# Prompt attention: bias addition and maximum in one VectorE operation (an addition with a running minimum, on negated queries and tables)

## The chip, the cores and the metric

The kernel runs on one core of one Trainium2 chip. The metric is the device time of one execution in microseconds (us), the median of several runs. The profile that is quoted below is of one further execution. TensorE is called PE in the profile, VectorE DVE, ScalarE ACT, GpSimd POOL and SyncE SP.

## What is computed

One inference step of a decoder trunk of one layer (model width 1024), for a prompt of 1024 tokens and for 8 sequences with 4 new tokens each, with shared weights. An input projection gives a convolution group, a pooling group, the queries of 8 heads of 64 (2 groups of 4 that share keys and values), and keys and values for three branches of attention: compressed blocks, selected blocks, and a sliding window of 512. The three are weighed by gates and added; then come an output projection, a SwiGLU block of width 2816 and the last norm. All of it is fp32.

The change is in the prompt's attention. There, for each block of 128 queries, head and branch:

```
s = einsum('bqgrd,bngd->bgrqn', q, k) * HEAD_DIM ** -0.5 + tbl[:, :, t5_bucket(dist)]
s = where(mask, s, -1e30);  p = softmax(s, axis=-1);  o = einsum(p, v)
```

`tbl` is a table of relative distances in 32 buckets; from a distance on, all keys share the last bucket, so after that bucket's value is subtracted everywhere (a softmax does not see it) only the last 256 keys of a row of scores need an addition. At 1024 tokens there are 16 blocks to select and 16 are selected, so the selected branch attends to every key up to the query's own.

## The kernel before

The program is written engine by engine; each engine's instructions run in the order in which they are written, and the engines wait for each other on semaphores. The stage that the change is about runs from some 398 to 735 us of the span, after the sample sequences' attention and before the output projection.

**Tiling.** The prompt has 8 blocks of 128 queries (`i` = 0 to 7). `ORDER` gives five groups of a block: head group 0 selected (`br` 1) and window (`br` 2), then the compressed branch of both head groups at once, then head group 1 selected and window. The four groups of `br` 1 and 2 are called dense; each has four jobs, one a head (`r`), 128 jobs in all. A job's scores are 128 queries by `w` keys: `w` = 128(i+1) in the selected branch, 128 min(i+1, 5) in the window. So 16 jobs (block 0) are 128 wide, 16 (block 1) 256 wide, and 96 wider; of these the window jobs of blocks 4 to 7 (32 jobs, 640 wide) also need the far edge of the window masked in their first 128 columns, with the table `tri`.

**A job's way.** TensorE multiplies queries by keys into PSUM (`p_score`, lines 878 and 879; `psA` and `psB` hold the scores in four banks, in turn). VectorE (`p_biased_max`, `biased_max`) adds the bias table `btab` to the last min(w, 256) columns and, where there is one, `tri` to the first 128 (line 1519), waits for its own last addition (`link`), and takes the negated maximum over all `w` columns into `nmax` (line 1523), which has four columns in turn and so waits for the exponential four jobs back. ScalarE (`p_exp`, line 1214) then computes exp(score + nmax) with the sum of the row on the side. When a group's four jobs are there, VectorE (`weigh`) turns the sums into factors, multiplies in the gates (lines 1599 and 1602) and scales the four tiles of probabilities (line 1607). TensorE transposes them (line 612) into `psC`, ScalarE copies them out (line 1111), and TensorE multiplies by the values (lines 893, 894 and 898) into `psD`. `steps()` sets the order on all three: the transposes and value products of group n - 3 lie between the scores of group n.

**The compressed branch** has one job a block: `c_center` adds its table, takes the maximum and subtracts it on VectorE (lines 1572, 1575 and 1576).

**GpSimd** splits keys and queries into a rounded part and a rest for TensorE (`split_keys`, `split_queries`, lines 1843 to 1860), a block ahead. Earlier it lays out the sample sequences' queries in `qbd` (line 1812).

**The samples' attention** uses the same `biased_max` (6 jobs) and stays as it is.

The waiting and the two operations of a job stand in:

```python
                for at, tab in adds:
                    n = tab.free_size()
                    op = dve.tensor_tensor(sc[:, at:at + n], sc[:, at:at + n], tab, ALU.add)
                link(op)
```

Of the kernel before, what the change touches and what calls it, by code (L numbers as in the profile page):

```python
# [17 lines left out]
ALU = mybir.AluOpType  # L18
ACT = mybir.ActivationFunctionType
AX = mybir.AxisListType.X  # L20

P = 128
D = 1024
T = 1024
NB, NS = 8, 4
# [16 lines left out]
EPS, NEG = 1e-6, -1e30  # L42
# [17 lines left out]
BAND = 3 * P  # L60
# [29 lines left out]
def constants():  # L90
    dist = np.concatenate([onehot(np.arange(DLO, DHI + 1)), onehot(2 * P - 1 - np.arange(BAND))], axis=1)
    c = np.zeros((P, C_END), np.float32)
    c[:, C_ID:C_ID + P] = np.eye(P)
    for t in range(NS):
        r = slice(32 * t, 32 * t + 32)
        c[r, C_OH:C_OH + 128] = onehot(PAST + t - (384 + np.arange(128)))[:32]
        c[r, C_OH + 128:C_OH + 160] = onehot(t - np.tile(np.arange(NS), NB))[:32]
        n = np.tile(np.arange(32), 4)
        o = onehot(PAST + t - (STRIDE * n + CBLK - 1))[:32]
        c[r, C_OH + 160:C_OH + 288] = o  # L100
    for row in range(P):
        b, h, t = row // 32, row // 4 % 8, row % 4
        for G in range(2):
            for col in range(32):
                if col // 4 != 4 * G + b or col % 4 > t:
                    c[row, C_MN + 32 * G + col] = NEG
            c[4 * 4 * G + 4 * b + t, C_SEL + 128 * G + row] = 1
        c[row, C_MW:C_MW + 4] = np.where(np.arange(4) <= t, NEG, 0)
        col = np.arange(128)
        c[row, C_MC:C_MC + 128] = np.where((col // 32 != b) | (col % 32 == 31), NEG, 0)  # L110
        for br in range(3):
            c[row, C_GM + 8 * br + h] = 1
    c[:, C_VA] = np.arange(P) >= CBLK - 1
    for k in range(2):
        w = np.where(np.arange(P) < 64, WINS[2 * k], WINS[2 * k + 1])
        c[:, C_IW + k] = 1.0 / w
        c[:, C_FX + 15 * k:C_FX + 15 * k + 15] = w[:, None] / np.minimum(w[:, None], np.arange(15)[None] + 1)
    tri = np.where(np.arange(P)[:, None] >= np.arange(P)[None, :], NEG, 0).astype(np.float32)
    return {"c_dist": dist, "c_pack": c, "c_tri": tri}


# [109 lines left out]
def build(nc, A, out):  # L231
    ctx = ExitStack()
    with ctx:
# [93 lines left out]
        small2 = at("small2", [P, 64], 228864)  # L327
        psums = [small2[:, 4 * k:4 * k + 4] for k in range(4)]
        precs = [small2[:, 16 + 4 * k:20 + 4 * k] for k in range(4)]
        cmax, csum, crec = small2[:, 32:40], small2[:, 40:48], small2[:, 48:56]  # L330
        sprob = [narrow[:, WP[2] * k:WP[2] * k + WP[2]] for k in range(2)]
        kpT = [narrow[:, 2 * WP[2] + 512 * k:2 * WP[2] + 512 * k + 512] for k in range(2)]
# [685 lines left out]
        def _(sc_):  # L1018
# [29 lines left out]
            for m in range(NU):  # L1048
# [3 lines left out]
                for n, (c0, w) in enumerate(chunks):  # L1052
                    sc_.wait_ge(s["z_mm"], 3 * m + n + 1)
                    b = bank[3 * (m % 2) + n]
                    if m in (0, 2):
                        if m == 2 and n == 0:
                            sc_.wait_ge(s["glu_done"], 1)
                        op = sc_.activation(sig[:, c0:c0 + w], b[:, 0:w], ACT.Sigmoid)
                    elif m < U_Q:
                        for lo, hi, dst in ext_cols(uex, m - 4, c0, w, PB, UE, PB):  # L1060
                            srcap = b[:, lo:hi]
                            if lo:
                                srcap = srcap.rearrange("p (b t) -> p b t", t=NS)
                            op = sc_.copy(dst, srcap)
                    elif m < U_K:
                        op = sc_.mul(qT[:, m - U_Q, c0:c0 + w], b[:, 0:w], HD ** -0.5)
                    elif m < U_G:
                        if m == U_V and n == 0:
                            sc_.wait_ge(s["fvec_out"], 16)
                        dst = (keysC, keysT, valsT)[(m - U_K) // 2][:, (m - U_K) % 2]  # L1070
                        op = sc_.copy(dst[:, c0:c0 + w], b[:, 0:w])
                    else:
                        op = sc_.activation(gatesT[0:3 * NH, c0:c0 + w], b[0:3 * NH, 0:w], ACT.Sigmoid)
# [121 lines left out]
            def p_exp(n, r):  # L1195
                job = NSJ + JOB[n, r]
                w = g_width(n)
                sc_.wait_ge(s["score_in"], job + 1)
                if n >= PSETS:
                    old = n - PSETS  # L1200
                    sc_.wait_ge(s["turn_fill"], UNIT[("t", old, len(g_tiles(old)) - 1)] + 1)
                elif n == 0 and r == 0:
                    sc_.wait_ge(s["out_done"], 2)
                if n not in DENSE:
                    if n < PSETS:
                        sc_.wait_ge(s["prob_zero"], 1)
                    sc_.activation(pcmp[:, :, :, 0:w].rearrange("p r g n -> p (r g) n"),
                                   p_scores(n, r).rearrange("p (x n) -> p x n", n=HD)[:, :, 0:w], ACT.Exp
                                   ).then_inc(s["exp_done"], 1)
                    return  # L1210
                q = DENSE[n]
                if r == 0 and q >= 4:
                    sc_.wait_ge(s["sum_read"], q - 3)
                sc_.activation(prob(n, r)[:, 0:w], p_scores(n, r)[:, 0:w], ACT.Exp,
                               bias=nmax[:, job % 4:job % 4 + 1], accum_out=psums[q % 4][:, r:r + 1]).then_inc(s["exp_done"], 1)

            def out_half(i, g):

# [105 lines left out]
        def _(dve):  # L1324
# [12 lines left out]
            def tables():  # L1337

                dve.wait_ge(s["table_mm"], 1)
                dve.tensor_copy(fvec, bank[0][0:NH, 0:BAND]).then_inc(s["fvec_ev"], 1)  # L1340
                dve.wait_ge(s["table_mm"], 2)
                dve.wait_ge(s["state_turn"], 1)
                dve.tensor_copy(ctab[:, :, :], bank[1][:, 0:CMPN * NH].rearrange("p (c h) -> p h c", h=NH)
# [148 lines left out]
            for kv, dst in ((0, kcT), (1, vcT)):  # L1492
# [4 lines left out]
                if kv == 0:  # L1497
                    for g in range(KVH):
                        gp = slice(HD * g, HD * g + HD)
                        dve.tensor_scalar(kcBD[gp, HD * g:HD * g + NCMP], bank[kv][gp, NB * 32:NB * 32 + NCMP],  # L1500
                                          posk[gp, kv:kv + 1], None, ALU.add)
                dve.tensor_scalar(dst[:, :], bank[kv][:, 0:KC_N - 1], posk[:, kv:kv + 1], None, ALU.add
                                  ).then_inc(s["cmp_ev"], 1)
            dve.wait_ge(s["gate_mm"], 1)
# [50 lines left out]
            def p_biased_max(n, r):  # L1555
                i, g, br = GROUPS[n]
                w, h = g_width(n), GQ * g + r
                m = min(w, 256)
                adds = [(w - m, btab[:, h, 256 - m:])]
                if br == 2 and i >= 4:  # L1560
                    adds.append((0, tri[:, :]))
                biased_max(NSJ + JOB[n, r], p_scores(n, r), w, adds)

            def c_center(n):

# [163 lines left out]
        def _(pool):  # L1729
# [76 lines left out]
            for g in range(KVH):  # L1806
                gp = slice(HD * g, HD * g + HD)
                for G in range(2):
                    for b_ in range(4):
                        dst = qbd[gp, G, 32 * b_ + 16 * g:32 * b_ + 16 * g + 16].rearrange("p (r t) -> p r t", t=NS)  # L1810
                        at = T + 16 * G + NS * b_
                        op = pool.tensor_copy(dst, qT[gp, :, at:at + NS])
            op.then_inc(s["qbd_done"], 1)

            pool.wait_ge(s["kvt_a"], NT + 1)
# [100 lines left out]
```

## Time and profile before

| | |
|---|---|
| median of 3 runs | 1679.63 us (1677.31 to 1681.72) |
| the profiled execution | 1680.7 us; span of its profile 1678.6 us |
| mean granted TensorE clock | 0.962 of full speed |
| busy: PE, DVE, ACT, POOL | 1522.3 us (91%), 769.6 us (46%), 477.7 us (28%), 140.9 us (8%) |
| DMA | 89.08 MB, mean 53 GB/s |

A group of the profile shows a line, an engine, an operation, the tiles out<-in, the count, the busy time and the mean of one, and then how long the engine sat idle just before them and what released it. Busy time on PE counts overlapping matmuls once, and their ends are modelled. The chain of waits follows the work that ended last back from its end; "issue" in it is time in which an engine waited for nothing that the profile shows.

### The profile page before, as it was taken

To read this page: it belongs to the slowest core of one execution; us is meant where nothing else is said; L and a number is where in the kernel's file an instruction comes from. 1 tells how busy PE (TensorE), PEld (TensorE's weight loads), DVE (VectorE), ACT (ScalarE), POOL (GpSimd) and SP (SyncE) were. 2 spreads that over 40 slices of the span, in tenths; PEclk is the share of its full clock that TensorE was granted. 3 is DMA by queue.
4 is the path that set the end of the run, shared out by engine and by line. 5 is a ranking of instruction groups with operands and counts; after the bars stand their busy time and mean duration, and the time that the engine had idled before them with its cause. 6 is when DMAs were issued, how large, how long until landed. Compare 5 with 4: busy or idle time off the path is not lost.

```text
span 1678.6 us, 22817 instructions
## 1 busy us (share of the span) xinstructions
PE 1522.3 (91%) x8812; PEld 1366.6 (81%) x8812; DVE 769.6 (46%) x1416; ACT 477.7 (28%) x978; POOL 140.9 (8%) x212
## 2 busy tenths in 40 slices
PE   4899996897788888989979999999999999999994
PEld 3899985655456555669969999999999999999994
DVE  4359834015987776632252143341423414243157
ACT  3212212333555555541142111111111112111112
POOL 1001202304322220000020000000000000000002
PEclk9899998998999998989979999999999999999997
DMA  7631202640000000041101020211202112021113
GB/s 181 160 74 51 56 1 76 187 154 1 1 1 1 1 1 1 23 144 46 43 0 51 23 69 18 64 49 31 66 20 61 48 35 67 17 63 48 36 38 120
DMA packets 140216, 89.08 MB, mean 53 GB/s; under 512 B 33314, under 2 KB 135289, under 8 KB 140033
## 3 DMA queue, kind: packets, MB, share of 16 engines
q1 hardware_dynamic: 137617, 78.74, 16.5%
q0 software_dynamic: 2496, 8.88, 2.0%
q8 instruction: 76, 1.25, 0.3%
q14 instruction: 27, 0.22, 0.0%
HBM read 78.85 MB, written 13.19 MB: 55 GB/s over the span
## 4 chain that ended last, share of the span: by engine, by line
PE 79%; DVE 11%; issue 4%; ACT 3%; DMA 1%; SPq 1%; POOL 1%; DVEq 0%; ACTq 0%; POOLq 0%
PE psC L925 17%; PE psA L925 17%; PE psB L925 16%; PE psD L898 5%; PE psC L612 4%; PE psA L654 4%; PE psB L654 3%; PE psC L654 3%; DVE wide L1607 2%; PE psD L612 2%; PE psA L776 1%; DVE nmax L1523 1%; DVE psB L1519 1%; PE psA L878 1%; PE psB L878 1%
## 5 line engine op out<-in xcount | busy, mean ns | idle before, releaser
L1624 DVE TENSOR_TENSOR wL<-wraw,wH 128x1024 fp32r<-128x1024 f32 (+1 forms) x140 | 100.3, 717 | 223.9 <-ACT wH L1229 223.8
L898 PE MATMUL psD<-probTb,kvtok 128*128 128x512 f32 x264 | 138.4, 607 | 18.0 <-ACT probTb L1111 18.0
L1229 ACT CAST wH<-wraw 128x1024 fp32r<-128x1024 f32 (+1 forms) x140 | 90.2, 648 | 200.0 <-PE psC L925 93.8
L925 PE MATMUL psA<-fH,wH 128*128 128x352 f32 x416 | 139.2, 335 | 4.2 <-DVE fL L1658 3.5
L925 PE MATMUL psA<-fL,wH 128*128 128x352 f32 x416 | 135.7, 326 | 0.0
L925 PE MATMUL psB<-fH,wH 128*128 128x352 f32 x416 | 134.5, 323 | 1.2 <-DVE fL L1674 1.2
L925 PE MATMUL psA<-fH,wL 128*128 128x352 f32 x416 | 135.5, 326 | 0.0
L925 PE MATMUL psC<-fH,wH 128*128 128x352 f32 x416 | 134.2, 323 | 0.0
L925 PE MATMUL psB<-fH,wL 128*128 128x352 f32 x416 | 133.5, 321 | 0.0
L925 PE MATMUL psC<-fL,wH 128*128 128x352 f32 x416 | 133.4, 321 | 0.0
L925 PE MATMUL psC<-fH,wL 128*128 128x352 f32 x416 | 133.4, 321 | 0.0
L925 PE MATMUL psB<-fL,wH 128*128 128x352 f32 x416 | 133.3, 320 | 0.0
L1755 POOL TENSOR_TENSOR small<-small 128x1 f32<-128x1 f32 (+1 forms) x27 | 18.6, 692 | 1038.7 <-DVE small L1371 1038.6
L1111 ACT COPY probTb<-psC 128x512 f32<-128x512 f32 (+2 forms) x150 | 85.1, 570 | 56.4 <-PE psC L612 56.2
L1694 DVE TENSOR_TENSOR hid<-psB,hid 128x352 f32<-128x352 f32 x22 | 11.5, 525 | 192.5 <-PE psC L925 192.5
L1305 ACT CAST aH<-hid 128x352 fp32r<-128x352 f32 x66 | 30.7, 487 | 238.1 <-DVE hid L1694 238.1
L1442 DVE SCALAR_TENSOR_TENSOR ybuf<-glu,convw,ybuf 128x1296 f32<-128x1296 f32 x60 | 91.5, 1593 | 0.0
L925 PEld LDWEIGHTS psA<-fH,wH 128*128 128x128 f32 x416 | 79.9, 192 | 9.5 <-issue 6.6
L925 PEld LDWEIGHTS psA<-fL,wH 128*128 128x128 f32 x416 | 80.3, 193 | 0.0
L925 PEld LDWEIGHTS psA<-fH,wL 128*128 128x128 f32 x416 | 79.9, 192 | 0.0
L925 PEld LDWEIGHTS psB<-fH,wH 128*128 128x128 f32 x416 | 78.0, 188 | 1.3 <-issue 1.3
L925 PEld LDWEIGHTS psB<-fL,wH 128*128 128x128 f32 x416 | 78.2, 188 | 0.0
(337 smaller groups left out, 3608.2 us busy)
## 6 DMA issues: line engine op xcount, KB each, us to landing
wraw<-in_w_gu SPq DMA_DIRECT2D x44, 512.0 KB
wraw<-in_w_down SPq DMA_DIRECT2D x88, 128.0 KB
zraw<-in_w_in SPq DMA_DIRECT2D x12, 512.0 KB
xa<-in_x_prompt SPq DMA_DIRECT2D x8, 512.0 KB, 9.8
pages<-in_cache_cmp_kv SPq DMA_DIRECT2D x32, 128.0 KB, 2.3
xt<-in_x_prompt SPq DMA_DIRECT2D x8, 512.0 KB, 6.5
out_y_prompt<-featT SPq DMA_DIRECT2D x8, 512.0 KB, 2.6
out_new_win_sample<-in_cache_win_kv POOLq DMA_DIRECT2D x1, 4064.0 KB, 22.7
```

The lines of the kernel that those rows point to most:

```text
L612: return pe.transpose(dst, src, ident[0:n, 0:n])
L654: mm = pe.matmul(bank[3 * (m % 2) + n][:, 0:w], wt[:, m % 2, k, :], mv[:, k, c0:c0 + w], start=(k == 0 and wt is zH and mv is xH), stop=(k ...
L878: pe.matmul(sc[:, c:c + half_w], qS[:, g, r, :], kH[:, br - 1, g, cols], start=True, stop=False)
L898: mm = pe.matmul(bank[6 + g], kvtok[:, kt, vc:vc + P], pt, start=(br == 1 and g == 0 and x == 0), stop=(br == 2 and g == 1 and x == len(g_ ...
L925: mm = pe.matmul(bank[3 * par + n][:, 0:cw], wt[:, par, k, :], mv[:, k, at:at + cw], start=(k == 0 and mv is mH and wt is wH), stop=(k == ...
L1111: op = sc_.copy(dst, srcfn(bank[4 + u % 2]))
L1229: sc_.copy(wH[:, par, 0:nk, :], wraw[:, par, 0:nk, :]).then_inc(s["wH_done"], 1)
L1305: sc_.copy(aH[:, par, x // 2, at:at + cw], hid[:, n, :]).then_inc(s["aH_done"], 1)
L1442: op = dve.scalar_tensor_tensor(out=y, in0=x, scalar=w, in1=y, op0=ALU.mult, op1=ALU.add)
L1607: dve.tensor_scalar(p, p, rc[:, r:r + 1], None, ALU.mult).then_inc(s["scaled"], 1)
L1624: dve.tensor_tensor(wL[:, par, 0:nk, :], wraw[:, par, 0:nk, :], wH[:, par, 0:nk, :].bitcast(F32), ALU.subtract).then_inc(s["wL_done"], 1)
L1755: pool.tensor_tensor(rstd[0:n, i:i + 1], ms[0:n, i:i + 1], mhalf[0:n, :], ALU.pow).then_inc(s[rs_], 1)
```

## The change

The queries are stored negated (ScalarE multiplies by minus the scale as it copies them out), and so are the bias table (negated as `fvec` is copied), the triangle `tri` (built on the host) and the compressed keys `kcBD` (a second operand of an operation that is there). GpSimd negates the samples' queries back as it lays out `qbd`. The dense scores in PSUM are thus minus the scores, the bias is added to them with one `tensor_tensor_reduce`, which writes the sums and, in the same operation, the running minimum over its 256 columns, started from a scalar. That minimum is what `nmax` held before: minus the maximum. ScalarE's exponential takes the scores with scale -1. Where a row is wider than 256, the minimum of its other columns is taken first (into one of two new columns `far`), waited for, and given as the scalar; the triangle, where there is one, is added and waited for before that.

```diff
--- before.py
+++ after.py
@@ -115,7 +115,7 @@
         w = np.where(np.arange(P) < 64, WINS[2 * k], WINS[2 * k + 1])
         c[:, C_IW + k] = 1.0 / w
         c[:, C_FX + 15 * k:C_FX + 15 * k + 15] = w[:, None] / np.minimum(w[:, None], np.arange(15)[None] + 1)
-    tri = np.where(np.arange(P)[:, None] >= np.arange(P)[None, :], NEG, 0).astype(np.float32)
+    tri = np.where(np.arange(P)[:, None] >= np.arange(P)[None, :], -NEG, 0).astype(np.float32)
     return {"c_dist": dist, "c_pack": c, "c_tri": tri}
 
 
@@ -327,6 +327,7 @@
         small2 = at("small2", [P, 64], 228864)
         psums = [small2[:, 4 * k:4 * k + 4] for k in range(4)]
         precs = [small2[:, 16 + 4 * k:20 + 4 * k] for k in range(4)]
+        far = small2[:, 56:58]
         cmax, csum, crec = small2[:, 32:40], small2[:, 40:48], small2[:, 48:56]
         sprob = [narrow[:, WP[2] * k:WP[2] * k + WP[2]] for k in range(2)]
         kpT = [narrow[:, 2 * WP[2] + 512 * k:2 * WP[2] + 512 * k + 512] for k in range(2)]
@@ -1063,7 +1064,7 @@
                                 srcap = srcap.rearrange("p (b t) -> p b t", t=NS)
                             op = sc_.copy(dst, srcap)
                     elif m < U_K:
-                        op = sc_.mul(qT[:, m - U_Q, c0:c0 + w], b[:, 0:w], HD ** -0.5)
+                        op = sc_.mul(qT[:, m - U_Q, c0:c0 + w], b[:, 0:w], -HD ** -0.5)
                     elif m < U_G:
                         if m == U_V and n == 0:
                             sc_.wait_ge(s["fvec_out"], 16)
@@ -1212,7 +1213,7 @@
                 if r == 0 and q >= 4:
                     sc_.wait_ge(s["sum_read"], q - 3)
                 sc_.activation(prob(n, r)[:, 0:w], p_scores(n, r)[:, 0:w], ACT.Exp,
-                               bias=nmax[:, job % 4:job % 4 + 1], accum_out=psums[q % 4][:, r:r + 1]).then_inc(s["exp_done"], 1)
+                               bias=nmax[:, job % 4:job % 4 + 1], scale=-1.0, accum_out=psums[q % 4][:, r:r + 1]).then_inc(s["exp_done"], 1)
 
             def out_half(i, g):
 
@@ -1337,7 +1338,7 @@
             def tables():
 
                 dve.wait_ge(s["table_mm"], 1)
-                dve.tensor_copy(fvec, bank[0][0:NH, 0:BAND]).then_inc(s["fvec_ev"], 1)
+                dve.tensor_scalar(fvec, bank[0][0:NH, 0:BAND], -1.0, None, ALU.mult).then_inc(s["fvec_ev"], 1)
                 dve.wait_ge(s["table_mm"], 2)
                 dve.wait_ge(s["state_turn"], 1)
                 dve.tensor_copy(ctab[:, :, :], bank[1][:, 0:CMPN * NH].rearrange("p (c h) -> p h c", h=NH)
@@ -1498,7 +1499,7 @@
                     for g in range(KVH):
                         gp = slice(HD * g, HD * g + HD)
                         dve.tensor_scalar(kcBD[gp, HD * g:HD * g + NCMP], bank[kv][gp, NB * 32:NB * 32 + NCMP],
-                                          posk[gp, kv:kv + 1], None, ALU.add)
+                                          posk[gp, kv:kv + 1], -1.0, ALU.add, ALU.mult)
                 dve.tensor_scalar(dst[:, :], bank[kv][:, 0:KC_N - 1], posk[:, kv:kv + 1], None, ALU.add
                                   ).then_inc(s["cmp_ev"], 1)
             dve.wait_ge(s["gate_mm"], 1)
@@ -1556,10 +1557,18 @@
                 i, g, br = GROUPS[n]
                 w, h = g_width(n), GQ * g + r
                 m = min(w, 256)
-                adds = [(w - m, btab[:, h, 256 - m:])]
+                job, sc = NSJ + JOB[n, r], p_scores(n, r)
+                low = sc[:, w - m:w]
+                dve.wait_ge(s["score_mm"], job + 1)
                 if br == 2 and i >= 4:
-                    adds.append((0, tri[:, :]))
-                biased_max(NSJ + JOB[n, r], p_scores(n, r), w, adds)
+                    link(dve.tensor_tensor(sc[:, 0:P], sc[:, 0:P], tri[:, :], ALU.add))
+                least = 3.0e38
+                if w > m:
+                    least = far[:, job % 2:job % 2 + 1]
+                    link(dve.tensor_reduce(least, sc[:, 0:w - m], AX, ALU.min))
+                dve.wait_ge(s["exp_done"], job - 3)
+                dve.tensor_tensor_reduce(out=low, in0=low, in1=btab[:, h, 256 - m:], scale=1.0, scalar=least, op0=ALU.add,
+                                         op1=ALU.min, accum_out=nmax[:, job % 4:job % 4 + 1]).then_inc(s["score_in"], 1)
 
             def c_center(n):
 
@@ -1809,7 +1818,7 @@
                     for b_ in range(4):
                         dst = qbd[gp, G, 32 * b_ + 16 * g:32 * b_ + 16 * g + 16].rearrange("p (r t) -> p r t", t=NS)
                         at = T + 16 * G + NS * b_
-                        op = pool.tensor_copy(dst, qT[gp, :, at:at + NS])
+                        op = pool.tensor_scalar(dst, qT[gp, :, at:at + NS], -1.0, None, ALU.mult)
             op.then_inc(s["qbd_done"], 1)
 
             pool.wait_ge(s["kvt_a"], NT + 1)
```

## Rows read from the trace of the kernel before

**Rows 1.** the page, the chain that ended last, its shares by engine.
```profile
PE 79%; DVE 11%; issue 4%; ACT 3%; DMA 1%; SPq 1%; POOL 1%; DVEq 0%; ACTq 0%; POOLq 0%
```

**Rows 2.** busy us of the engines, granted clock and DMA, in four stretches.
```profile
398.00:419.00 21.00, 15.42 (x72) 12.31 (x73) 18.06 (x68) 10.46 (x43) 9.57 (x16) 0.76 0.00 1
419.00:439.00 20.00, 15.22 (x76) 10.04 (x74) 19.18 (x56) 10.73 (x35) 7.07 (x9) 1.00 0.00 1
439.00:507.00 68.00, 53.78 (x238) 34.76 (x238) 58.97 (x131) 38.11 (x97) 16.57 (x24) 0.97 0.00 1
507.00:735.00 228.00, 202.11 (x920) 133.72 (x920) 153.47 (x297) 128.82 (x253) 29.34 (x36) 0.95 0.02 5
```

**Rows 3.** the chain by line in 398:439, 439:507 and 507:735 us.
```profile
by line: issue 22.5%; DVE wide L1607 11.7%; DVE psB L1519 11.7%; DVE psA L1519 9.7%; DVE nmax L1523 8.8%; DVE narrow L1607 6.9%; DVE small L1602 5.5%; PE psD L898 4.2%; ACT wide L1214 3.4%; PE psC L612 2.9%; DVE small L1599 2.2%; PE psA L87
by line: PE psD L898 23.1%; issue 18.2%; DVE wide L1607 10.2%; PE psC L612 9.0%; DVE narrow L1607 7.4%; DVE psB L1519 6.0%; DVE psA L1519 4.8%; DVE nmax L1523 4.5%; PE psA L879 2.8%; PE psA L878 2.7%; PE psB L879 2.2%; ACT probTb L1111 2.1%
by line: PE psD L898 29.1%; PE psC L612 14.5%; issue 9.8%; DVE wide L1607 8.8%; DVE nmax L1523 5.5%; PE psB L878 4.4%; PE psA L878 4.4%; PE psB L879 3.8%; PE psA L879 3.8%; PE psD L893 2.4%; DVE psA L1519 2.0%; DVE psB L1519 1.9%; PE psD L8
```

**Rows 4.** the chain in time: first and last of block 1's 16 additions.
```profile
415.89 0.22 DVE psA L1519
...
435.23 0.43 DVE psA L1519
```

**Rows 5.** VectorE groups, 398:735: shapes, count, busy us, mean ns, idle before.
```profile
L1519 DVE TENSOR_TENSOR psA<-psA,btab 128x256 f32<-128x256 f32 x56 | 23.9, 427 | 33.3 <-PE psA L879 33.0
L1519 DVE TENSOR_TENSOR psB<-psB,btab 128x256 f32<-128x256 f32 x56 | 23.9, 426 | 26.5 <-PE psB L879 26.4
L1519 DVE TENSOR_TENSOR psA<-psA,tri 128x128 f32<-128x128 f32 x16 | 4.6, 288 | 0.0
L1523 DVE TENSOR_REDUCE nmax<-psA 128x1 f32<-128x384 f32 x8 | 4.5, 557 | 0.3
```

**Rows 6.** VectorE in time (start, us, instruction): scores 256 wide.
```profile
430.29 0.42 DVE L1519 TENSOR_TENSOR psB<-psB,btab 128x256 f32<-128x256 f32 x1
430.75 0.42 DVE L1523 TENSOR_REDUCE nmax<-psB 128x1 f32<-128x256 f32 x1
431.09 0.42 DVE L1519 TENSOR_TENSOR psA<-psA,btab 128x256 f32<-128x256 f32 x1
```

**Rows 7.** the same view: scores 128 wide.
```profile
408.38 0.29 DVE L1519 TENSOR_TENSOR psB<-psB,btab 128x128 f32<-128x128 f32 x1
408.70 0.29 DVE L1523 TENSOR_REDUCE nmax<-psB 128x1 f32<-128x128 f32 x1
408.91 0.29 DVE L1519 TENSOR_TENSOR psB<-psB,btab 128x128 f32<-128x128 f32 x1
```

**Rows 8.** the same view: scores 640 wide, with the triangle.
```profile
524.11 0.42 DVE L1519 TENSOR_TENSOR psB<-psB,btab 128x256 f32<-128x256 f32 x1
524.44 0.28 DVE L1519 TENSOR_TENSOR psB<-psB,tri 128x128 f32<-128x128 f32 x1
524.76 0.83 DVE L1523 TENSOR_REDUCE nmax<-psB 128x1 f32<-128x640 f32 x1
525.50 0.22 DVE L1572 TENSOR_TENSOR psA<-psA,ctab 128x60 f32<-128x60 f32 x1
```

**Rows 9.** VectorE groups: three operations, two with a scalar read per partition.
```profile
L1442 DVE SCALAR_TENSOR_TENSOR ybuf<-glu,convw,ybuf 128x1296 f32<-128x1296 f32 x60 | 91.5, 1593 | 0.0
L1544 DVE SCALAR_TENSOR_TENSOR narrow<-psD,small,narrow 128x128 f32<-128x128 f32 x2 | 0.7, 351 | 0.1
...
L1624 DVE TENSOR_TENSOR wL<-wraw,wH 128x1024 fp32r<-128x1024 f32 x41 | 50.1, 1223 | 125.3 <-ACT wH L1229 125.3
```

**Rows 10.** ScalarE group, 398 to 735 us: reading its accumulator.
```profile
L1214 ACT ACTIVATION_READ_ACCUMULATOR narrow<-psA,nmax 128x1 f32 x32 | 6.3, 198 | 0.0
```

**Rows 11.** VectorE in order of time: two small additions, back to back.
```profile
427.14 0.34 DVE L1572 TENSOR_TENSOR psA<-psA,ctab 128x60 f32<-128x60 f32 x2
```

**Rows 12.** GpSimd, line 1812: min/median/max ns, first and last start.
```profile
L1812 POOL COPY qbd<-qT x16: 186/192/220, 300.6 to 302.7; 64x16 f32<-64x16 f32 x16
```

## Prediction

> **What bounds the kernel now.** I read the chain of waits first. Over the whole span 79% of it is PE and 11% DVE [rows 1], so VectorE work is worth something only where that 11% lies. The change touches the stage from 398 to 735 us, so I cut the busy times and the chain by stretch. From 398 to 439 us (blocks 0 and 1) DVE is busy 18.1 of 21 and 19.2 of 20 us, with PE at 15.4 and 15.2 [rows 2]; in the chain the line of the additions, L1519, has 21.4% and the maximum, L1523, 8.8% [rows 3]. From 439 to 507 us DVE is busy 59.0 of 68 us, and L1519's share is down to 10.8%. From 507 us on PE is busy 202 of 228 us and L1519 has 3.9% [rows 2, 3]. The reader is to see a stage whose limit moves: VectorE in the first two blocks, both engines in blocks 2 and 3, then TensorE, with VectorE late only at the start of a block. The additions themselves say the same: before those 256 wide DVE stood idle 59.8 us in all, for scores from PE [rows 5]. A saving in front of such an idle stretch is lost in it.
>
> So I count the jobs that are on the chain. Block 1: all 16, from 415.9 to 435.2 us, stand in the chain in order of time [rows 4]. In 398 to 439 us L1519 has 21.4% of 41 us, 8.8 us; the 16 of block 1 at about 0.40 us a piece take 6.4 of it, and the remaining 2.4 us at 0.29 are 8 jobs of block 0. In 439 to 507 us 10.8% of 68 us is 7.3 us, at 0.43 us 17 jobs. After 507 us 3.9% of 228 us is 8.9 us; reading it in time I find 7 window jobs with a triangle, 0.55 us each for their two additions, 3.9 us, and the other 5.0 us are 12 plain jobs. That is 8, 16, 29 (17 + 12) and 7 jobs.
>
> **What a job costs, before and after.** Start to start, a 256-wide job is 0.46 us (addition, with the wait for it) plus 0.34 (maximum) [rows 6]; a 128-wide one 0.32 + 0.21 [rows 7]; a 640-wide one with the triangle 0.33 + 0.32 + 0.74 [rows 8]. An operation that is waited for costs its duration plus some 0.03 us (0.427 against 0.46), one that is not some 0.08 less than its duration (0.83 against 0.74) [rows 5, 6, 8]. A maximum over 384 columns took 0.557 us against 0.83 over 640 [rows 5, 8]: 256 columns fewer are worth 0.27 us, 1.07 ns a column.
>
> The fused operation is not in this trace. I take it as an addition of its width whose end is not waited for, 0.34 us at 256 columns and 0.21 at 128 like the maximum there, plus two unknowns. First p, for a starting value read per partition (only where w is over 256): an operation with such a scalar took 351 ns at 128 columns against 288 without it [rows 9, 5], which gives 0.063. The other pair, 1296 columns in 1593 ns and 1024 in 1223 [rows 9], leaves up to 0.087 after 272 columns at 1.04 to 1.09 ns. Lower end 0. I take 0.063, the row that also reads PSUM. Second a, for getting the minimum out of the accumulator: ScalarE needs an instruction of its own for that, 0.198 us [rows 10], and that is the upper end; 0, if the value comes out with the operation, is the lower; a second small VectorE addition behind the first adds 0.12 us (0.34 for two [rows 11], 0.22 for one [rows 8]). I take 0.12, since it is VectorE's own. I see no reason for a negative p or a.
>
> The Trainium skill, "VectorE: DVE Perf Modes", section "Two Vector instructions with no wait between them", says that an operation that also writes out its accumulator is two instructions, the main one and an accumulator read. By that rule a = 0 is out; no VectorE row here shows it, and ScalarE's row is the nearest.
>
> Saved per job:
> - 128 wide: 0.53 before, 0.21 + a after: 0.32 - a = 0.20 (0.12 to 0.32).
> - 256 wide: 0.80 before, 0.34 + a after: 0.46 - a = 0.34 (0.26 to 0.46).
> - wider, no triangle: before 0.46 + d - 0.08 (d the full maximum's duration); after, the shorter maximum is waited for, d - 0.27 + 0.03, then 0.34 + p + a. Saved 0.28 - p - a = 0.09 (0 to 0.28).
> - with the triangle: before 0.33 + 0.32 + d - 0.08; after 0.32 + d - 0.27 + 0.03 + 0.34 + p + a, since the triangle's addition no longer runs beside another and two waits stand where one did. Saved 0.15 - p - a = -0.03, a small loss (-0.14 to 0.15).
>
> **The sum on the path.** Block 0: 8 x 0.20 = 1.6 us. Block 1: 16 x 0.34 = 5.4 us, but PE is busy 15.2 of 20 us there, so that stretch cannot give more than 4.8; I take 4.6. Plain wider jobs: 29 x 0.09 = 2.7 us. Triangles: 7 x 0.03 lost, 0.2. Together 8.7 us. Both ends: with p = a = 0, 2.6 + 4.8 + 8.0 + 1.0 = 16.4 us; with p = 0.087 and a = 0.198, 1.0 + 4.2 + 0 - 1.0 = 4.2 us. The other 68 of the 128 jobs are hidden by PE; if that cover went, they would add a few tenths.
>
> What is added beside it. The wait for `exp_done` stood before the maximum and now stands before the fused operation, with the same instructions behind it; the partial maximum is ahead of it. ScalarE's copy of the queries and its exponential keep their count and shape, only constants differ: 0. The bias copy becomes one operation with a constant, and `kcBD` gets a second operand in the same instruction: 0, at most a tenth of a us. GpSimd's 16 copies into `qbd` (0.19 us each, done at 302.9 us [rows 12]) become 16 multiplications; even at double the price they are 3 us longer, and the samples' first scores come some 40 us later, so they are hidden. Their cost shows only if the stores that GpSimd issues after them are then late, which nothing in this stage waits for. SP's queue is untouched until the last score: the loads of `w_out` start when it is done and so move up with it. Where the stall of block 1 goes, ScalarE's exponential and PE's value products are late next.
>
> **Rivals.**
> 1. The accumulator is dear (a near 0.2 or beyond, p at its end). Then only blocks 0 and 1 gain: the lower end above, 4.2 us or less, time 1675 to 1680. For it: ScalarE's 0.198. Against: VectorE's small operations are cheaper than ScalarE's.
> 2. The running minimum halves the fused operation's rate: one more 1.07 ns a column, 0.14 us at 128 columns and 0.27 at 256. Per job 0.06, 0.07, -0.18 and -0.30 are left; 8 x 0.06 + 16 x 0.07 - 29 x 0.18 - 7 x 0.30 = -5.7 us, a slower kernel at 1685, and more where jobs that PE hides come out of cover. It decides from some 0.17 us extra a fused operation on: 8.7 us over 52 jobs on the path (block 0's counted half). Against it: an operation with two SBUF inputs ran 1296 columns in 1593 ns [rows 9], full rate, though without an accumulator, and here only one input is in SBUF.
> 3. TensorE takes over at once. If the score and value products of blocks 0 and 1 are the second limit already, block 1 gives 3 rather than 4.6 us and the rest half: about 5.5 us, time 1674. For it: PE's 15.2 of 20 us, and a granted clock of 0.76 in 398 to 419 us [rows 2], which makes PE's part of block 0 longer. Against: at 75% busy PE also waits for VectorE.
> 4. The change does nothing to be measured, because fewer instructions are offset by the extra waits: the plain and triangle jobs at 0, block 0 and 1 in other idle time.
>
> The Trainium skill, "Vector Engine (DVE) Microarchitecture Reference", section "Points that are easy to get wrong", says that an instruction of the scalar-tensor-tensor family with two SBUF sources not in bf16 runs at half rate, as no read port is left for reading back the accumulator. By it the time would be rival 2's only if it also held for one PSUM and one SBUF source; the trace's two-source row ran at full rate, and no row has an accumulator.
>
> **How the numbers follow.** The terms come from one execution: 1680.7 us, of which its profile's span is 1678.6. That is 1.1 us over the median of 1679.63. The forecast is 1680.7 - 8.7 = 1672.0 in its terms, 1670.9 against the median. A measurement of this kernel tells about 0.3%, 5 us, from no change. Forecast (5 to 16 us gained) 0.60; rival 1 (0 to 5 us) 0.15; rival 2 0.13; rival 3 0.09, most of it still over 5 us; rival 4 0.03. Faster by over 0.3%: 0.60 + 0.08 = 0.68. Within: 0.15 + 0.03 + 0.01 + 0.01 (a mild case of rival 2) = 0.20. Slower: 0.12. The range from 1662 to 1681 holds the forecast up to nearly its cheap end, and rivals 1, 3 and 4; it leaves out rival 2 and the last of the cheap end.
>
> **What would show it.** The fused group in the changed trace: some 0.43 us at 256 columns (0.29 at 128), whether with an accumulator read behind it, and about 0.06 us more in the wide jobs. Start to start in block 1, 0.46 us a job in place of 0.80. Busy DVE time of 398 to 735 us down by 16 x 0.20 + 16 x 0.34 + 64 x 0.09 - 32 x 0.03, some 13 us. Blocks 0 and 1 over about 6 us sooner, blocks 2 and 3 another 1.5, and hardly more afterwards; the rest of the kernel unchanged. A fused operation of 0.6 us or more at 256 columns would make the prediction wrong, and so would an unchanged block 1.

## The result and the profile after

The changed kernel takes 1667.34 us (median of 6 executions, 1660.29 to 1671.11) against 1680.36 for the kernel before on the same chip; the ratio is 0.9918, 95% interval 0.9893 to 0.9944, that is 9 to 18 us less. Two more series of six gave 0.9908 (0.9882 to 0.9934) and 0.9921 (0.9893 to 0.9949). Over the 18 executions the mean is 1665.5 us, 14 to 15 us under the kernel before. It was forecast at 1670.9, 8.7 us less. Direction, order and range held; the gain is some 1.6 times what was forecast.

I measure the stage from the first dense score product to the first product of the output projection. Before it took 337.6 us (398.7 to 736.3), with the change 324.1, 324.5 and 324.4 in three profiles: 13.1 to 13.5 us less. The profiled executions are not average ones: they took 1660.3, 1663.2 and 1659.2 us, and their spans are 17 to 21 us shorter than the one before. Most of what the stage does not explain lies in the unchanged code after it, which took 936.6, 936.4 and 937.4 us against 942.2 before; in the nine other profiles of this document it took 936.6 once and 940.6 to 943.6 otherwise. How much of that the change causes is not shown, so the stage is the firmer measure.

The page's chain by engine has hardly moved, as against [rows 1]:

```profile
PE 78%; DVE 11%; issue 4%; ACT 4%; DMA 1%; POOL 1%; SPq 1%; DVEq 0%; ACTq 0%; POOLq 0%
```

Busy time by stretch (stretch, its length, then PE, weight loads, DVE, ACT, POOL, granted clock, DMA share, GB/s), cut by time near the stretches of [rows 2], the last ones 11 and 14 us earlier:

```profile
397.00:418.00 21.00, 14.98 (x76) 11.43 (x76) 16.84 (x76) 10.54 (x47) 10.98 (x17) 0.84 0.00 1
418.00:438.00 20.00, 17.63 (x93) 12.38 (x91) 17.98 (x64) 12.43 (x40) 9.92 (x15) 1.00 0.00 1
438.00:496.00 58.00, 49.14 (x218) 31.81 (x218) 46.52 (x145) 34.67 (x87) 13.17 (x17) 0.97 0.00 1
496.00:721.00 225.00, 199.52 (x920) 132.54 (x920) 146.64 (x363) 129.39 (x253) 29.02 (x36) 0.96 0.02 6
```

The second row is again a cut of 20 us, but now holds part of block 2's work beside block 1's: PE is busy 17.6 of 20 us in place of 15.2, DVE 18.0 in place of 19.2. The chain by line, in blocks 0 and 1 (397 to 440 us) and in blocks 4 to 7 (504 to 721 us):

```profile
by line: issue 20.5%; DVE wide L1616 11.4%; PE psD L899 10.6%; DVE narrow L1616 9.5%; ACT wide L1215 6.4%; PE psC L613 5.8%; DVE nmax L1570 4.0%; DVE psA L1570 3.8%; DVE psB L1570 3.5%; DVE small L1611 3.1%; ACT narrow L1215 3.0%; PE psA L8
by line: PE psD L899 30.7%; PE psC L613 14.8%; DVE wide L1616 10.7%; issue 7.6%; DVE small L1568 5.3%; PE psA L879 4.2%; PE psA L880 3.8%; PE psB L879 3.8%; PE psB L880 3.5%; PE psD L894 2.0%; DMA wraw<-in_w_out 1.7%; ACT probTb L1112 1.7%;
```

In the first, the addition and maximum had 30.2% between them [rows 3]; the fused line L1570 has 11.3%. In the second, the partial minimum (L1568) has 5.3% where the full maximum had 5.5%.

VectorE's groups (shapes, count, busy us, mean ns, idle before them), which answer to [rows 5] and [rows 9]:

```profile
L1570 DVE CUSTOM_DVE_ANT_0 psA<-psA,btab,small 128x256 f32<-128x256 f32 x48 | 23.7, 493 | 1.7
L1570 DVE DVE_READ_ACCUMULATOR2_ANT nmax<- 128x1 f32 x128 | 18.1, 142 | 0.0
L1568 DVE TENSOR_REDUCE small<-psA 128x1 f32<-128x384 f32 x20 | 11.1, 557 | 2.7 <-PE psA L880 2.0
L1564 DVE TENSOR_TENSOR psA<-psA,tri 128x128 f32<-128x128 f32 x16 | 4.8, 301 | 12.1 <-PE psA L880 12.1
L1570 DVE CUSTOM_DVE_ANT_0 psA<-psA,btab 128x256 f32<-128x256 f32 x8 | 3.5, 444 | 0.0
```

The fused operation appears as `CUSTOM_DVE_ANT_0` with an accumulator read behind each of the 128. With a constant to start from it takes 0.444 us at 256 columns, with a value per partition 0.493: p is 0.05 in the durations. The read lasts 0.142 us. What it costs is seen only in order of time. Four instructions of block 1, the answer to [rows 6]:

```profile
425.35 0.43 DVE L1570 CUSTOM_DVE_ANT_0 psB<-psB,btab 128x256 f32<-128x256 f32 x1
425.69 0.15 DVE L1570 DVE_READ_ACCUMULATOR2_ANT nmax<- 128x1 f32 x1
425.69 0.47 DVE L1570 CUSTOM_DVE_ANT_0 psB<-psB,btab 128x256 f32<-128x256 f32 x1
426.07 0.15 DVE L1570 DVE_READ_ACCUMULATOR2_ANT nmax<- 128x1 f32 x1
```

The read starts 0.34 us after the fused operation, and the next fused operation starts in the same hundredth as the read: they overlap. It then lasts 0.47 in place of 0.43 us, and the jobs are 0.38 us apart, where they were 0.80. So a is 0.04 before another fused operation, and near nothing before others. At 128 columns the jobs are 0.25 us apart (0.53 before [rows 7]):

```profile
406.15 0.29 DVE L1570 CUSTOM_DVE_ANT_0 psA<-psA,btab 128x128 f32<-128x128 f32 x1
406.36 0.14 DVE L1570 DVE_READ_ACCUMULATOR2_ANT nmax<- 128x1 f32 x1
406.36 0.33 DVE L1570 CUSTOM_DVE_ANT_0 psB<-psB,btab 128x128 f32<-128x128 f32 x1
406.61 0.14 DVE L1570 DVE_READ_ACCUMULATOR2_ANT nmax<- 128x1 f32 x1
```

A 768-wide job of the selected branch and then a window job with the triangle, the answer to [rows 8]:

```profile
547.86 0.68 DVE L1568 TENSOR_REDUCE small<-psA 128x1 f32<-128x512 f32 x1
548.57 0.49 DVE L1570 CUSTOM_DVE_ANT_0 psA<-psA,btab,small 128x256 f32<-128x256 f32 x1
548.98 0.14 DVE L1570 DVE_READ_ACCUMULATOR2_ANT nmax<- 128x1 f32 x1
548.98 0.33 DVE L1564 TENSOR_TENSOR psB<-psB,tri 128x128 f32<-128x128 f32 x1
549.34 0.56 DVE L1568 TENSOR_REDUCE small<-psB 128x1 f32<-128x384 f32 x1
549.94 0.49 DVE L1570 CUSTOM_DVE_ANT_0 psB<-psB,btab,small 128x256 f32<-128x256 f32 x1
550.35 0.14 DVE L1570 DVE_READ_ACCUMULATOR2_ANT nmax<- 128x1 f32 x1
```

The wide job is 0.71 + 0.41 = 1.12 us; before it was 0.46 + 0.88 (its maximum took 0.96 us, in the row below, and by [rows 8] some 0.08 of that runs beside the next operation) = 1.34: 0.22 saved. The triangle job is 0.36 + 0.60 + 0.41 = 1.37 with the overlap of the operation before it, and 1.32 us without that; before it was 1.39: 0.02 to 0.07 saved, not 0.03 lost.

```profile
L1523 DVE TENSOR_REDUCE nmax<-psB 128x1 f32<-128x768 f32 x4 | 3.8, 958 | 0.1
```

GpSimd's 16 multiplications into `qbd` took 0.25 us in place of 0.19 [rows 12] and ended at 303.7 us, with the samples' first scores at 348:

```profile
L1821 POOL TENSOR_SCALAR qbd<-qT x16: 242/250/270, 299.4 to 303.4; 64x16 f32<-64x16 f32 x16
```

### The profile page after: what moved, and what is told of

Read it like the earlier page. It is cut to its first block, busy times and chain, and to the rows that moved or that the text cites. A ratio compares the mean times of both kernels' runs of the same rounds, so it can differ in the third digit from the quotient of the medians.

```text
span 1658.4 us, 22913 instructions
## 1 busy us (share of the span) xinstructions
PE 1511.9 (91%) x8812; PEld 1358.7 (82%) x8812; DVE 747.6 (45%) x1512; ACT 476.1 (29%) x978; POOL 143.1 (9%) x212
## 4 chain that ended last, share of the span: by engine, by line
PE 78%; DVE 11%; issue 4%; ACT 4%; DMA 1%; POOL 1%; SPq 1%; DVEq 0%; ACTq 0%; POOLq 0%
PE psC L926 17%; PE psB L926 16%; PE psA L926 16%; PE psD L899 5%; PE psC L613 4%; PE psA L655 4%; PE psB L655 4%; PE psC L655 3%; DVE wide L1616 2%; PE psD L613 2%; PE psA L777 1%; DVE small L1568 1%; PE psA L879 1%; DVE ybuf L1443 1%; PE psA L880 1%
```

## The experiments

All are the changed kernel with one edit. "Early" is the stretch from block 0's compressed job to block 2's (the end of block 0, block 1, half of block 2), "late" the one from there to block 7's; both are cut at the start of line 1572's addition, or of what that line has become, and the stage is as above. Stage, early, late and half speed are us of the one profiled execution. Half speed is the time in the stage that the granted clock was at 1.2 GHz rather than 2.4. Each ratio is against the kernel before in the same series, whose median was between 1678.2 and 1681.8 us; the first row has one of them.

| kernel | ratio (95% interval) | median us | stage | early | late | half speed |
|---|---|---|---|---|---|---|
| before | 1 | 1679.6 | 337.6 | 48.3 | 226.5 | 38 |
| the change | 0.9918, 0.9908, 0.9921 | 1667.3, 1663.7, 1664.7 | 324.1 to 324.5 | 42.1 | 220.9, 221.4, 221.3 | 27, 31, 31 |
| two operations, all negated | 1.0 (0.9977 to 1.0023) | 1681.5 | 337.5 | 48.3 | 226.4 | 38 |
| fused to 256 wide | 0.9955 (0.9932 to 0.9978) | 1672.1 | 334.7 | 43.9 | 229.4 | 44 |
| fused above 256 | 0.9951 (0.9929 to 0.9972) | 1673.0 | 333.6 | 46.6 | 224.1 | 41 |
| fused in block 1 | 0.9979 (0.9961 to 0.9996) | 1677.0 | 334.5 | 42.2 | 229.0 | 51 |
| change + one addition a job | 0.9955 (0.9929 to 0.9981) | 1675.0 | 336.9 | 44.9 | 228.0 | 41 |
| change + one fill a job | 0.9944 (0.9923 to 0.9965) | 1671.0 | 331.0 | 42.0 | 227.6 | 38 |
| change + two fills a job | 0.9947 (0.9926 to 0.9969) | 1671.6 | 334.2 | 42.5 | 229.8 | 48 |
| near maximum, two operations | 0.9913 (0.9888 to 0.9937) | 1665.1 | 320.6 | 46.9 | 211.1 | 28 |
| near maximum, fused | 0.9714 (0.9691 to 0.9737) | 1633.9 | 293.5 | 38.1 | 192.9 | 10 |

**Is it the fusing?** Everything else of the change was kept and only the two operations were put back, ahead of the fused one, which is then never reached (`...` marks lines left out, the triangle's addition):

```diff
+                if True:
+                    op = dve.tensor_tensor(low, low, btab[:, h, 256 - m:], ALU.add)
+                    ...
+                    link(op)
+                    dve.wait_ge(s["exp_done"], job - 3)
+                    dve.tensor_reduce(nmax[:, job % 4:job % 4 + 1], sc[:, 0:w], AX, ALU.min).then_inc(s["score_in"], 1)
+                    return
```

> Everything of the change but the fusing: queries, tables and compressed keys negated, exponential with scale -1, but per job one addition to the last 256 columns (and the triangle), one wait and one minimum over all columns, as before. Theory: the stage's gain is made by the fused operation alone, so the stage (first dense score product to first product of the output projection, 337.6 us before, 324.1 with the change) comes out at 337.6 within 1.5 us and the time at 1680. Rival: part of the gain is the sign flips' (another exponential, another order of instructions): the stage is shorter than 336.

The ratio is 1.0, to within 4 us, and the stage 337.5: signs, scale and tables cost and bring nothing that shows. The rival falls.

**Which jobs?** The same edit with another condition in place of `True`: on the width, on the width the other way round, and on the block:

```diff
+                if w > 256:      # then w <= 256, then i != 1: these jobs in two operations
```

> The fused operation only where a job is at most 256 wide (the 32 jobs of blocks 0 and 1); wider jobs as before. Theory (each job on the path saves what its own operations lose: 0.28 us at 128 columns, 0.42 at 256, capped by TensorE in block 1): the stage is 7 us shorter, about 330.6, all of it ahead of block 2's compressed job; blocks 3 to 7 take as long as before, within 0.3 us each; time about 1673. Rival (the 1.1 us that each of the later blocks gained is handed on from the early start, by GpSimd's splits or the weights' loads): blocks 3 to 7 are 1 us shorter here too, and the stage is at 324 to 326.

> The other half: the fused operation only where a job is wider than 256 (96 jobs of blocks 2 to 7); blocks 0 and 1 as before. Theory (29 plain wide jobs on the path save 0.22 us each, the 7 with a triangle nothing): the stage is 6.4 us shorter, about 331.2, with blocks 0 and 1 as before and about 1.1 us less in each later block; time about 1673.5. Rival (handed on from the early start): the later blocks gain nothing, stage at 337. By the forecast's own numbers (0.09 us a job) it would be 2.5 us shorter, 335.

> The fused operation in block 1 alone (16 jobs, 256 wide), all others with two operations. Each saves 0.42 us start to start, 6.7 us in all. Theory (TensorE's 15.2 busy of 20 us caps it): 4.8 us, 1675.5. Rival (no cap): 6.7 us, 1673.5. The profile should show VectorE idle before some of these jobs, for TensorE's scores, where it was never idle before.

The two halves are worth 0.45% and 0.49% and add up to the change's 0.8 to 0.9%; the times came out as expected (1672.1 and 1673.0). The stages did not: 2.9 and 4.0 us shorter, not 7 and 6.4. (In the profiled execution with narrow jobs fused, 5.6 us more were saved in the unchanged code after the stage.) The windows say where the rest is. Early and late stretch, for fused to 256 wide, fused above 256, and fused in block 1:

```profile
400.90:444.80 43.90, 32.90 (x162) 23.32 (x162) 38.48 (x131) 23.79 (x81) 20.06 (x28) 0.92 0.00 1
444.80:674.20 229.40, 201.33 (x893) 134.89 (x894) 173.56 (x349) 128.11 (x271) 39.66 (x50) 0.92 0.00 1
```

```profile
403.80:450.40 46.60, 33.50 (x162) 23.27 (x160) 43.36 (x136) 24.22 (x81) 17.88 (x26) 0.93 0.00 1
450.40:674.50 224.10, 198.76 (x893) 133.09 (x894) 162.70 (x429) 127.58 (x271) 39.62 (x50) 0.93 0.00 1
```

```profile
407.90:450.10 42.20, 33.14 (x157) 23.91 (x156) 37.74 (x129) 23.93 (x81) 17.99 (x26) 0.87 0.00 1
450.10:679.10 229.00, 202.22 (x899) 135.19 (x899) 173.60 (x349) 128.06 (x271) 39.84 (x51) 0.92 0.00 1
```

With narrow jobs fused the early stretch is 4.4 us shorter (and what lies ahead of it in the stage 1.9 us), and the late one, whose VectorE instructions are those of the kernel before, is 2.9 us longer, with DVE busy about as long (173.6 against 172.5 us) but PE 201.3 against 197.4, at a clock of 0.92 where before had:

```profile
405.60:453.90 48.30, 33.59 (x162) 23.37 (x160) 45.07 (x129) 24.32 (x81) 17.90 (x26) 0.93 0.00 1
453.90:680.40 226.50, 197.40 (x893) 132.61 (x894) 172.54 (x350) 128.06 (x271) 39.55 (x50) 0.94 0.00 1
```

So no gain was handed on to the later blocks; some was lost there again, with more of the time at half speed (38 us of the late stretch against 27 before). With only block 1 fused the early stretch is 6.1 us shorter, of the 6.7 that 16 jobs of 0.42 us make: TensorE did not cap it at 4.8. The late stretch gave 2.5 of it back, at 0.92 again. The whole time (0.7 to 6.6 us less by its interval) does not decide between 4.8 and 6.7; the early stretch does.

Fusing block 0 as well brought almost nothing more. From the stage's start to block 2's compressed job the kernel before takes 55.2 us, the one with block 1 fused 49.1, and the one with blocks 0 and 1 fused 48.9, where 8 jobs of 0.28 us would make 2.2 more. About as much went into the scaling of the probabilities (line 1607 before, 1624 in these two), 18.8 against 16.5 us, although the granted clock was the higher one, 0.93 against 0.86. VectorE's busy time of that line alone, from the stage's start to block 2's compressed job: before, blocks 0 and 1 fused, block 1 fused:

```profile
398.70:453.90 55.20, 17.04 (x36) 0.91 0.00 1
395.90:444.80 48.90, 18.81 (x36) 0.93 0.00 1
401.00:450.10 49.10, 16.54 (x36) 0.86 0.00 1
```

With block 0 done sooner, its scaling falls beside GpSimd's split of the queries. Scaling a 128x128 tile takes 0.27 to 0.29 us where GpSimd is idle; beside one of its operations it can take far more, here 2.03 us for three tiles, the last of them 1.28 us and over just after GpSimd's:

```profile
402.43 2.03 DVE L1624 TENSOR_SCALAR narrow<-narrow,small 128x128 f32<-128x128 f32 x3
403.06 1.32 POOL L1877 TENSOR_TENSOR qS<-qT,qS 64x512 fp32r<-64x512 f32 x1
```

The change itself shows the same 1.8 us later (GpSimd's operation 1.32 us, the tile beside it 1.28).

**How much of VectorE's time counts?**

```diff
+                dve.tensor_tensor(small2[:, 58 + job % 6:59 + job % 6], cpk[:, 0:1], cpk[:, 1:2], ALU.add)
```

> The change, with one more VectorE addition of a single column, waited for by nobody, behind each of the 128 fused operations (it leaves nothing out). Its price start to start is some 0.1 us. Theory (60 of the 128 jobs lie on the path): the stage is 6 us longer than with the change, 330. Rival (all of VectorE's time counts in this stage): 12.8 us longer, 337. Rival (TensorE sets the stage by now): under 2 us longer, 326.

The time rose by 6 to 9 us over the change and the stage by 12.5, which is the rival's number. But the addition was not as small as meant (min, median and max ns, first and last start):

```profile
L1572 DVE TENSOR_TENSOR small<-cpk x128: 148/156/957, 401.8 to 713.0; 128x1 f32<-128x1 f32 x128
```

It mostly starts 0.07 us ahead of the next operation, yet 19 of the 128 lasted over 0.2 us, up to 0.96. Each of the 19 ran beside a GpSimd operation and ended 9 to 20 ns after that one did; of the 109 short ones 5 did run beside one. So the rival's number is met by an experiment that added more than it meant to. To take that away, the addition was replaced by one fill, then two:

```diff
+                dve.memset(small2[:, 58 + job % 6:59 + job % 6], 0.0)
```

> The change, with one fill of a single column on VectorE behind each of the 128 fused operations, in place of the small addition of e4 (which read two SBUF operands and sometimes took 0.4 to 0.96 us beside GpSimd's operations). Some 0.06 us each, 7.7 us of VectorE in all. Theory (60 of 128 jobs on the path, as counted in the chain): 4 us over the change. Rival (nearly all VectorE time counts, as e4's 12.8 us for 10.6 us of it seemed to say): 7 us or more.

> The same with two such fills a job. Theory: 8 us over the change, and the stage's gain gone by about half. Rival: 14 us or more, no faster than the kernel before. If the step from one fill to two costs more than the step from none to one, the half-speed clock is what multiplies it.

> The change, as the measure beside these two: 1664 to 1667 us, stage 324 to 325 us.

Against the change in the same series (mean 1664.4 us) one fill costs 5 us (mean 1669.8) and two cost 7 (1671.0), each to within 3 or 4 us, where the theory had 4 and 8 and the rival 7 and 14. One fill does not decide between them; two speak against the rival. In the profiles the stage rose by 6.6 and 9.8 us, and neither theory explains how. The two stretches, of the change and of one fill:

```profile
400.50:442.60 42.10, 32.86 (x162) 23.29 (x162) 36.67 (x139) 23.78 (x81) 20.08 (x28) 0.92 0.00 1
442.60:663.90 221.30, 195.58 (x893) 131.95 (x894) 161.35 (x431) 127.60 (x271) 39.55 (x50) 0.95 0.00 1
```

```profile
401.50:443.50 42.00, 32.65 (x162) 23.25 (x162) 36.99 (x171) 23.83 (x81) 20.02 (x28) 0.94 0.00 1
443.50:671.10 227.60, 199.46 (x893) 133.88 (x894) 163.07 (x511) 127.91 (x271) 39.48 (x50) 0.93 0.00 1
```

The early stretch is the same (42.1 and 42.0 us), so a fill behind a job costs next to nothing where VectorE sets the pace. The late one is 6.3 us longer, although DVE was busy only 1.7 us longer there; PE's busy time rose by 3.9 us, at a clock of 0.93 in place of 0.95. Of the late stretch 31 us are at half speed with one fill, and 20 to 24 with the change; as half speed can cost no more than half of its time, that is worth 3.4 to 5 of the 6.3 us at most. Another 1.3 us stand in the scaling between the compressed jobs of blocks 2 and 3 (11.3 us in place of 9.9 to 10.2), where one more tile meets GpSimd's split. With two fills the late stretch is 229.8 us, 38 of them at half speed; with block 1 or the narrow jobs fused, whose late instructions are those of the kernel before, it is 229.0 and 229.4 us, also with 38, against the 226.5 with 27 of the kernel before. So small changes ahead of or in this stretch made it 2 to 9 us longer, and TensorE's time at half speed moved with it. What is cause and what is effect there is not settled, nor why the change has the shortest of these in all three profiles.

**Is TensorE the limit from block 2 on?** Shifting a softmax by the maximum of the last 256 columns gives the same result as long as nothing overflows, so the partial minimum can go. In the fused kernel the triangle's addition then also needs no wait:

```diff
-                    link(dve.tensor_tensor(sc[:, 0:P], sc[:, 0:P], tri[:, :], ALU.add))
+                    dve.tensor_tensor(sc[:, 0:P], sc[:, 0:P], tri[:, :], ALU.add)
...
-                if w > m:
-                    least = far[:, job % 2:job % 2 + 1]
-                    link(dve.tensor_reduce(least, sc[:, 0:w - m], AX, ALU.min))
```

The one that is not fused has the additions, one wait and `tensor_reduce` over the last 256 columns alone.

> The change without the minimum over the columns beyond the last 256: the softmax is shifted by the maximum of the last 256 columns alone (any shift gives the same softmax as long as nothing overflows), so the fused operation starts from a constant, the partial minimum and its wait go, and the triangle's addition is waited for by nobody. Theory: per plain wide job on the path 0.4 to 0.9 us less than with the change, per triangle job 0.7, that is some 20 us of VectorE, of which TensorE leaves about half: 10 us under the change, some 1657, with VectorE idle before most fused operations of blocks 4 to 7. And the fused operation with a constant takes 0.44 us in place of 0.49. Rival (from block 2 on TensorE and the half-speed clock set the pace already): under 3 us less than the change, 1664 or more.

> Not fused: per job one addition to the last 256 columns (and the triangle), one wait, and a minimum over the last 256 columns alone, negated as in the change. The shift is that of the last 256 columns. Theory: a job is 0.46 + 0.34 us as in block 1 before, so blocks 0 and 1 gain nothing and the wide jobs 0.27 to 0.8 us each on the path: between the change and the version with both, about 1665; the fused operation is worth 7 to 10 us on top. Rival: the length of the maximum is what counts, fusing nothing: then this equals the version with both within 2 us.

> The change once more, for a time with more executions and as the measure for the others of this series. By the sums of the two halves measured one at a time (1672.7 and 1672.9 us on average, 7.8 and 7.6 us under the kernel before): 1665 to 1668 us.

The fused one is at 1633.88 us, ratio 0.9714: some 48 us under the kernel before and 31 under the change, three times what I expected. The one with two operations is at 1665.05, as expected, level with the change; but fusing was to be worth 7 to 10 us on top of it and is worth 31. Its stretches, and those of the fused one:

```profile
403.20:450.10 46.90, 37.69 (x162) 25.98 (x160) 43.67 (x129) 24.41 (x81) 18.02 (x25) 0.82 0.00 1
450.10:661.20 211.10, 188.72 (x890) 127.23 (x891) 141.18 (x350) 127.23 (x272) 38.83 (x50) 0.98 0.00 1
```

```profile
400.80:438.90 38.10, 31.48 (x157) 22.67 (x158) 32.60 (x131) 23.56 (x81) 19.28 (x28) 0.91 0.00 1
438.90:631.80 192.90, 185.47 (x897) 125.56 (x896) 105.12 (x350) 127.12 (x273) 39.52 (x51) 1.00 0.00 1
```

In the fused one PE is busy 185.5 of 192.9 us in the late stretch at full clock: now TensorE is the limit. With two operations it is 188.7 of 211.1. My "TensorE leaves about half" was wrong, and so was the 20 us that it halved: the gain over the change is 31. If the 60 jobs that were on the path before are still the ones that count, the fusing is worth 8 x 0.28 + 52 x 0.42 = 24.1 us there; the stages differ by 27.1, but there are also 17 us less at half speed, worth up to 8.7, so the agreement may be partly chance. The fused operation with a constant takes 0.431 us, as thought:

```profile
L1567 DVE CUSTOM_DVE_ANT_0 psA<-psA,btab 128x256 f32<-128x256 f32 x56 | 24.1, 431 | 36.0 <-PE psA L880 34.6 <-ACT wide L1215 1.4
```

This version beats both kernels. It is bought with a condition: a score further than 256 keys back may exceed the largest of the near ones by no more than some 88, the logarithm of the largest fp32 number, or exp overflows. With the inputs here nothing overflowed; other inputs were not tried.

## Why the prediction was right, and where it was off

The forecast of 8.7 us rests on a price too high for the accumulator read and on a cap that did not hold, which made it too low; it had no term for the clock and none for the scaling beside GpSimd. The direction and the place of the gain were right by reasoning, the distance to the measured 13 to 15 us is the balance of these.

**The limit that moves** held: the gain is in the stage, with most of it early. Between the compressed jobs of blocks 0 and 1, 1 and 2, and so on, the blocks took 21.5, 26.8, 32.4, 39.2, 47.8, 51.4 and 55.8 us before and 20.3, 21.8, 31.4, 38.2, 46.6, 50.3 and 54.6 with the change. I had written "hardly more afterwards"; from block 2's compressed job on each step gave about 1.1 us. They have the plain wide jobs that I had counted on the path there, and each was worth more than I thought.

**The mis-sized term is a**, the accumulator read: 0.12 us in the forecast, 0 to 0.04 measured. I priced it as a second small operation in the queue; it runs beside the next operation. That it would come as two instructions was right; that a = 0 was out by that did not follow. In the sum a is 0.08 us or more for each of 60 jobs on the path, some 5 us. That is about what the forecast missed, but no run separates it, and the clock below is worth as much. ScalarE's 0.198 us, my upper end, was no guide for VectorE: its read lasts 0.142 us, most of it or all hidden.

**The other terms.** p was 0.063, measured 0.05 in the duration and 0.07 start to start: right. The plain wide job: 0.09 forecast, 0.22 measured; the triangle job: -0.03, measured +0.02 to 0.07; both follow from a. Block 1's cap by TensorE (4.6 of 5.4 us) was wrong: 6.1 of 6.7 us arrived with block 1 alone, at a PE busy share of 76% before. With the measured prices the sum is 8 x 0.28 + 16 x 0.42 + 29 x 0.22 + 7 x 0.05 = 15.7 us, against 13.3 in the stage and 14 to 15 in the time; block 0's 2.2 us of it hardly arrived. (Rival 2's threshold divides by 52 jobs; with block 0's counted half they are 56, and it is 0.155 us, not 0.17.) VectorE's busy time in the stage fell by 22.1 us (250.4 to 228.3), where I had 13.

**The rivals.** The dear accumulator fell with the overlap. The halved rate fell: 0.444 us at 256 columns against 0.302 at 128 is 1.1 ns a column, the rate of the plain addition. TensorE taking over at once fell with block 1 alone and with the two kernels with the near maximum. What no rival had is the clock: in the stage TensorE was at half speed for 38 us before and 27 to 31 with the change, and 10 in the fastest version. Those 7 to 10 us less are worth at most half of their length, 3.4 to 5.1 us; PE's busy time in the stage, for the same products, fell by as much, from 286.4 to 281.2 and 282.3 us. So 3 to 5 of the 13.3 us may have come by the clock, and then 8 to 10 are VectorE's own savings, nearer to the 8.7 of the forecast than its terms deserve: a part of its closeness is luck. Whether an earlier VectorE is what keeps TensorE at full speed is not shown: with the halves fused alone half speed rose, to 44 and 41 us, and with block 1 alone to 51.

## What to carry to other kernels

Fusing a reduction into the elementwise pass before it pays where VectorE is late, for the jobs that stand in the chain of waits; count them there rather than from busy shares, and expect less than price times count (13.3 of 15.7 us here). Look also at what the engine will meet when it comes earlier: here some 2 us more of scaling beside GpSimd. Price a helper instruction such as an accumulator read by how far apart the jobs start, not by its duration. And ask whether the reduction's whole range is needed: here up to three quarters of a wide row's maximum were only for safety, and leaving them out brought another 31 us.

## What the runs showed of the hardware

- A VectorE operation with an accumulator output is two instructions in the profile: 0.42 to 0.49 us for 256 columns from PSUM and a 0.14 us read that starts 0.34 us after it (0.41 with a starting value per partition) and overlaps the next operation.
- A small fill (0.059 us) on VectorE that delayed nothing in the early stretch went with a late stretch 6.3 us longer, with TensorE at 0.93 rather than 0.95 of its clock. Half speed in that stretch was 7 to 10 us longer, worth up to 5 us, so a part of this kernel worth less than that is better read from a stretch that ends before it than from the whole time.
- A VectorE scaling of a 128x128 tile took 0.27 to 0.29 us with GpSimd idle and up to 1.3 us beside one of its operations.
- Additions of one column with two operands in SBUF lasted 0.156 us in the median and up to 0.96 beside GpSimd's work, where the 19 long ones ended 9 to 20 ns after GpSimd's operation; a fill of the same column took 0.059 us in all 128 cases:

```profile
L1572 DVE MEMSET small<- x128: 59/59/59, 397.3 to 703.2; 128x1 f32 x128
```
